# Four taps of the 31-tap convolution in each TensorE product instead of two, the taps divided anew over the engines, and the kernel's opening reordered

## The reference

```python
def pool_mixer(h, w, b, scale):               # windows 2, 4, 8, 16: running mean minus the value itself
    csum = jnp.cumsum(hf, axis=1)
    ...
        mean = (c - lo) / count[None, :, None]
        outs.append(mean - hf[..., sl])
    p = jnp.stack(outs, axis=2).astype(h.dtype)
    y = jnp.einsum('bsgc,gcd->bsgd', p, w) + b
    return y.reshape(B, S, D) * scale

def conformer_conv(x, w_in, b_in, conv_w, conv_b, ln_g, ln_b, w_out, b_out):
    a, g = jnp.split(x @ w_in + b_in, 2, axis=-1)
    h = a * jax.nn.sigmoid(g)
    h = lax.conv_general_dilated(             # depthwise, 31 taps, causal, 1024 channels
        h, conv_w[:, None, :].astype(h.dtype), window_strides=(1,),
        padding=[(CONV_KERNEL - 1, 0)],
        dimension_numbers=("NWC", "WIO", "NWC"),
        feature_group_count=D_MODEL) + conv_b
    h = jax.nn.silu(layer_norm(h, ln_g, ln_b))
    return h @ w_out + b_out
```

## Time and profile before

| | |
|---|---|
| median of 3 runs | 1448.52 us |
| profiled execution | 1448.29 us |
| its span (first to last instruction) | 1446.5 us |
| TensorE busy / VectorE / ScalarE / GpSimd | 1437.2 / 921.2 / 637.3 / 204.8 us |
| convolution stage, 929.4 to 1040 us: busy of the same four | 109.79 / 106.03 / 99.21 / 96.55 us of 110.6 |
| its DMA share (mean busy share of 16 engines) | 0.71 |

### The profile page before, as it was taken

How to read it: one execution, slowest core, us unless ns; L and a number is a source line. 1 busy time by engine, 2 the same in 40 slices (tenths; PEclk the granted TensorE clock), 3 DMA queues, 4 the chain that set the end, 5 groups by cost and what they waited for, 6 DMA issues and landing times.

```text
span 1446.5 us, 19954 instructions
## 1 busy us (share of the span) xinstructions
PE 1437.2 (99%) x6828; PEld 1172.1 (81%) x6828; DVE 921.2 (64%) x1339; ACT 637.3 (44%) x994; POOL 204.8 (14%) x162
## 2 busy tenths in 40 slices
PE   9999999999999999999999999999999999999999
PEld 8788888888887898888888888766588888888887
DVE  7877773573645667777754755899988653544532
ACT  7444442342546675444422434798754321222210
POOL 4000000000302232000000003599511000000000
PEclk9999999999999999999999999999999999999999
DMA  5223223222322112232232232387613332222321
GB/s 191 88 99 104 87 102 116 73 102 91 121 90 71 30 60 81 96 108 94 91 125 75 88 108 81 101 186 179 161 45 102 116 101 89 100 102 88 102 94 51
DMA packets 44413, 144.34 MB, mean 100 GB/s; under 512 B 5184, under 2 KB 6208, under 8 KB 44352
## 3 DMA queue, kind: packets, MB, share of 16 engines
q1 hardware_dynamic: 41200, 133.79, 28.0%
q0 software_dynamic: 2016, 7.34, 2.8%
q10 hardware_dynamic: 1136, 2.42, 0.4%
HBM read 137.19 MB, written 2.10 MB: 96 GB/s over the span
## 4 chain that ended last, share of the span: by engine, by line
PE 94%; DVE 2%; ACT 1%; DMA 1%; issue 1%; POOL 1%; SPq 0%; ACTq 0%; DVEq 0%; POOLq 0%
PE bank L594 29%; PE bank L595 29%; PE bank L596 29%; PE bank L867 2%; PE bank L742 1%; PE bank L770 1%; PE bank L755 1%; DVE bank L1689 1%; PE bank L877 0%; DMA cst<-cst_in 0%; DMA shifted<-hc 0%; PE bank L922 0%; PE bank L923 0%; PE bank L635 0%; PE bank L926 0%
## 5 line engine op out<-in xcount | busy, mean ns | idle before, releaser
L594 PE MATMUL bank<-xh,whi 128*128 128x512 f32 x1184 | 464.9, 393 | 0.8 <-DVE wlo L1340 0.6
L596 PE MATMUL bank<-xh,wlo 128*128 128x512 f32 x1184 | 460.9, 389 | 0.0
L595 PE MATMUL bank<-xl,whi 128*128 128x512 f32 x1184 | 460.8, 389 | 0.0
L945 ACT ACTIVATE whi<-raw 128x1024 fp32r<-128x1024 f32 x244 | 255.8, 1050 | 238.7 <-PE bank L596 236.0
L1340 DVE TENSOR_TENSOR wlo<-raw,whi 128x1024 fp32r<-128x1024 f32 x230 | 288.0, 1252 | 43.8 <-ACT whi L945 35.9
L594 PEld LDWEIGHTS bank<-xh,whi 128*128 128x128 f32 x1184 | 222.2, 188 | 55.4 <-issue 7.1
L595 PEld LDWEIGHTS bank<-xl,whi 128*128 128x128 f32 x1184 | 222.3, 188 | 46.6 <-issue 1.2
L596 PEld LDWEIGHTS bank<-xh,wlo 128*128 128x128 f32 x1184 | 222.3, 188 | 46.4
L594 PE MATMUL bank<-ahi,whi 128*128 128x512 f32 x608 | 236.5, 389 | 0.0
L595 PE MATMUL bank<-alo,whi 128*128 128x512 f32 x608 | 236.5, 389 | 0.0
L596 PE MATMUL bank<-ahi,wlo 128*128 128x512 f32 x608 | 236.5, 389 | 0.0
(11 more groups left out here) (191 smaller groups left out, 1344.6 us busy)
## 6 DMA issues: line engine op xcount, KB each, us to landing
raw<-w_ffn_up SPq DMA_DIRECT2D x88, 512.0 KB, 3.3
raw<-w_ffn_down SPq DMA_DIRECT2D x32, 512.0 KB, 3.2
raw<-w_mlp_up SPq DMA_DIRECT2D x32, 512.0 KB, 3.2
raw<-w_mlp_down SPq DMA_DIRECT2D x32, 512.0 KB, 3.2
raw<-w_ain SPq DMA_DIRECT2D x16, 512.0 KB, 3.4
raw<-w_ffn_down SPq DMA_DIRECT2D x16, 384.0 KB, 3.0
raw<-w_qkv SPq DMA_DIRECT2D x12, 512.0 KB, 3.2
wlo<-w_ain POOLq DMA_DIRECT2D x10, 512.0 KB, 7.3
```

The source lines that it names most:

```text
L594: nc.tensor.matmul(out_, hi, mh, start=first, stop=False)
L595: nc.tensor.matmul(out_, hi, ml, start=False, stop=False)
L596: return nc.tensor.matmul(out_, lo, mh, start=False, stop=last)
L945: nc.scalar.activation(whi[:, s, 0:tiles * P], raw[:, s, 0:tiles * P], ACT.Copy)\
```

## The change

1. **TensorE's products** hold four taps: 32 channels, four times on the partitions, each copy one token later. A round is four matmuls of 32 output columns, for four taps of 128 channels. Taps on TensorE go from 68 to 92 and rounds from 34 to 23 (4, 3, 3, 2, 3, 3, 7, 9 become 2, 2, 2, 2, 2, 3, 5, 5).
2. **The shifted copies** of a chunk are still four DMAs, one per group of 32 channels; each reads its 32 rows four times, overlapping, and writes all 128 partitions: 512 runs of some 2 KB instead of 256.
3. **The diagonals** are made by VectorE, one instruction per chunk, from a table `pair_w4` that 16 DMAs of short runs (17 numbers, 68 bytes) write before the attention; before, ScalarE did it in 68 instructions.
4. **The taps** elsewhere: own 56 to 51, late 52 to 42, GpSimd's 72 to 63. The last `gated` stands behind all taps of its round and `collect(5)`. Places of the adding DMAs move.
5. **`statistics`** is four matmuls of 32 columns over half the tokens each, instead of two of 64 over all.
6. **The opening**: no products with zeros, the window matrices made on GpSimd without the constants' DMA, the residual's bias on GpSimd, two loads moved from ScalarE's queue to SP's, `weigh_pooled` on VectorE no longer waiting for ScalarE's half, 8 instead of 10 warm-up products, two splits moved.

```diff
-PE_TAPS = (8, 6, 6, 4, 6, 6, 14, 18)
-SHIFTS = 2
-GROUP = P // SHIFTS
+PE_TAPS = (8, 8, 8, 8, 8, 12, 20, 20)
+SHIFTS = (4,) * C
+GROUP = tuple(P // s for s in SHIFTS)
+ROUNDS = tuple(n // s for n, s in zip(PE_TAPS, SHIFTS))
...
-DIAGS = 3
-POOL_TAPS = (11, 10, 9, 9, 9, 9, 8, 7)
-LATE_TAPS = (0, 6, 8, 11, 11, 12, 4, 0)
-LATE_START = (2, 2, 2, 0, 0, 0, 0, 4)
+DIAGS = 2
+POOL_TAPS = (10, 9, 9, 8, 8, 8, 7, 4)
+LATE_TAPS = (2, 4, 6, 9, 12, 9, 0, 0)
+LATE_START = (2, 2, 2, 0, 0, 0, 0, 0)
...
-LOW_AT = {... 17: (7, 3), 18: (7, 6), 19: (7, 6)}
+LOW_AT = {... 17: (6, 5), 18: (7, 1), 19: (7, 3)}
...
-WARM = 10
+WARM = 8
@@ load_pairs
+                    for s in range(shifts):
+                        for g in range(shifts):
+                            src = vec_in[g * group:(g + 1) * group, w:w + C * TAPS].rearrange("p (c k) -> p c k", c=C)
+                            sp.dma_start(pair_w[shifts][s:P:shifts, g], src[:, lo:hi, s:s + n]).then_inc(pairs_loaded, 16)
@@ shift_hc
-                for g in range(SHIFTS):
-                    for s in range(SHIFTS):
-                        sp.dma_start(shifted[s * GROUP:(s + 1) * GROUP, c % 2, g, 0:n],
-                                     hc[g * GROUP:(g + 1) * GROUP, c % HC, s:s + n]).then_inc(hc_shifted[c % 2], 16)
+                for g in range(SHIFTS[c]):
+                    window = hc[g * group:(g + 1) * group, c % HC, 0:n]
+                    taps = bass.AP(window.tensor, window.offset, [window.ap[0], (1, SHIFTS[c]), (1, n)])
+                    sp.dma_start(shifted[:, c % 2, g, 0:n], taps).then_inc(hc_shifted[c % 2], 16)
@@ SP's loads of the opening
+                    sp.dma_start(res[:, 6:8, :], xT[:, 6:8, :]).then_inc(x_in[3], 16)
+                    sp.dma_start(vec[:, head:], vec_in[:, head:]).then_inc(vec_loaded, 16)
@@ GpSimd
+            for c in range(C):
+                pool.wait_ge(chain_done, 2 * (c // 2) + 2)
+                nc.gpsimd.tensor_scalar(res[:, c, :], res[:, c, :], col(pbs, c), None, ALU.add).then_inc(res_biased, 1)
@@ window_mean
-                nc.tensor.matmul(bank[BAND_BANKS[c]][:], zero[:, 0:P], zero[:], start=True, stop=False)
...
-                                          start=False, stop=(b == NBLK - 1))
+                                          start=(b == 0), stop=(b == NBLK - 1), skip_group_check=True)
@@ convolve
+                for q in range(ROUNDS[c]):
+                    for g in range(SHIFTS[c]):
+                        rows, at = slice(g * group, (g + 1) * group), SHIFTS[c] * q
+                        mm = nc.tensor.matmul(bank[6 + b][rows, :], dg[:, c % DIAGS, q, rows],
+                                              shifted[:, b, g, at:at + T],
+                                              start=(q == 0), stop=(q == ROUNDS[c] - 1))
@@ statistics
+                for j, x in enumerate((hv[:, c, :], sq[:, c % 2, :])):
+                    for h in range(2):
+                        rows, at = slice((2 * j + h) * QUADRANT, (2 * j + h + 1) * QUADRANT), slice(h * T // 2, (h + 1) * T // 2)
+                        mm = nc.tensor.matmul(norm[0][rows, at], ones[:, 0:QUADRANT], x[:, at],
+                                              start=(c == 0), stop=(c == C - 1))
@@ VectorE, once per chunk behind gated(c)
+                V.tensor_tensor(dg[:, c % DIAGS, 0:rounds].rearrange("p q (g n) -> p q g n", g=shifts),
+                                pair_id[shifts][:].rearrange("p (q g n) -> p q g n", q=1, g=1).broadcast_to(shape),
+                                w.rearrange("p g (q n) -> p q g n", n=1).broadcast_to(shape), ALU.mult)\
+                    .then_inc(diag_ready, 1)
...
-                    if n == gated_at and c == C - 2:
-                        gated(C - 1)
...
+                if c == C - 2:
+                    gated(C - 1)
```

More of the change, by code:

```diff
@@ L188, in build @@
             wg = sb("wg", [P, 4, 2, 2 * P], F32, own)
-            near = sb("near", [P, 5, PAD + P + PAD], F32, own)
+            near = sb("near", [P, 5, P + PAD], F32, own)
             mix = sb("mix", [P, 2, 4, P + PAD], F32, own)
             mixed = sb("mixed", [P, NBLK, 4, P + PAD], F32, own)
-            zero = sb("zero", [P, T], F32R, own)
             pick = sb("pick", [P, NBLK, NBLK], F32, own)
@@ L997, in step @@
                             k = 2 * b + j
-                            split_hi(p.unit, i, k + AHEAD)
-                            if first and isinstance(i, int) and i == 0 and k == 0:
+                            opening = first and isinstance(i, int) and i == 0
+                            if not (opening and k == 1):
+                                split_hi(p.unit, i, k + AHEAD)
+                            if opening and k == 0:
                                 root(first)
+                                split_hi(p.unit, i, 1 + AHEAD)
                             par = VEC["glu"] + ((layer * FF_PAIRS + q0) * 2 + k) * 4 + 16 * i
@@ L1218, in _ @@
             p = ph["ain"]
-            def diagonals(c, part=0, parts=1):
-                if c >= DIAGS and part == 0:
-                    act.wait_ge(conv_done, c - DIAGS + 1)
-                if c == 0:
-                    act.wait_ge(pairs_loaded, 16 * SHIFTS * (SHIFTS + 1))
-                pairs = PE_TAPS[c] // SHIFTS
-                for q in range(part * pairs // parts, (part + 1) * pairs // parts):
-                    e = c * TAPS + SHIFTS * q
-                    for g in range(SHIFTS):
-                        last = nc.scalar.activation(dg[:, c % DIAGS, q, g, :], pair_id[:], ACT.Copy,
-                                                    scale=pair_w[:, g, e:e + 1])
-                if part == parts - 1:
-                    last.then_inc(diag_ready, 1)
             def products(c, ks):
@@ L1400, in step @@
                         par = VEC["glu"] + ((layer * FF_PAIRS + q0) * 2 + 2 * b) * 4 + 16 * i
+                        opening = first and isinstance(i, int) and i == 0 and b == 0
                         split_lo(p.unit, i, 2 * b + AHEAD)
-                        if first and isinstance(i, int) and i == 0 and b == 0:
+                        if opening:
                             invert(first, rinv_count)
@@ L1414, in step @@
                                                        op0=ALU.mult, op1=ALU.add).then_inc(done, 1)
[L1415 removed]
+                        if not opening:
+                            split_lo(p.unit, i, 2 * b + 1 + AHEAD)
                         dve.wait_ge(gate_ready, pair + 1)
@@ L1531, in add_pooled @@
                                        op0=ALU.mult, op1=ALU.add).then_inc(pooled, 1)
-            for g in range(4):
-                weigh_pooled(g)
+            weigh_pooled(0)
+            window_weights()
+            weigh_pooled(1)
+            first_window_weights()
+            weigh_pooled(2)
+            weigh_pooled(3)
             evict_pooled(0)
@@ L1543, in _ @@
             V.tensor_tensor(square_of(4), square_of(4), square_of(0), ALU.add).then_inc(all_summed, 1)
-            window_weights()
-            split_lo(0, 0, 4)
+            for m in range(C):
+                for half in range(2):
+                    h = C * (m // REP) + REP * half + m % REP
+                    made = V.memset(qs[HD * half:HD * (half + 1), m:m + 1], HD ** -0.5 / SLOPE[h])
+            made.then_inc(q_scales, 1)
             dve.wait_ge(rms_ready, 1)
@@ L1756, in _ @@
                 gate_at = next((n for n in range(rounds) if issued[n] >= GATE_AT), rounds - 1)
-                gated_at = next((n for n in range(rounds) if issued[n] >= LAST_GATED), rounds - 1)
                 for n in range(rounds):
```

180 lines of the change are left out of this document (82 added, 98 removed).

## The result

The changed kernel takes 1457.61 us (median of 4 runs, 1454.63 to 1459.89) beside 1448.53 us for the kernel before: a ratio of 1.0057, with a 95% interval of 1.0044 to 1.0070. It is slower by 6 to 10 us, where 1440.9 was forecast. The profiled run is its fastest, 1454.63 us with a span of 1452.6, so the trace explains 6.1 us more of span than before; the rest of the median's distance lies in how the other runs vary.

What follows compares the result with a forecast made beforehand. TensorE was busy 1437.2 of 1446.5 us, but the convolution stage's end hung on VectorE, four DMAs, `convolve(7)` and the last statistics. 1448.5 - 3.8 (stage) - 3.8 (opening) = 1440.9; range 1436.0 to 1446.5, the forecast's own 1437.5 to 1443.5.

Steps and rivals of the forecast that it cites:

- The bound of before: End of the convolution stage: the path is VectorE, four DMAs, `convolve(7)`, the last statistics.
- A round at 0.85 us: TensorE's convolution: four column groups run at once, so 23 rounds cost 19.6 us, 9.4 less than the old 34.
- VectorE up to `gated(7)`: Convolution stage: taps -5.5, `collect(5)` +1.4, diagonals +5.1, waits for TensorE -1.3; sum -0.3 us.
- The copies of chunk 7: Ahead of `convolve(7)`: twice the bytes in twice the runs, +2.2 us, landing at 1031.6; bounds +0 and +5.
- The last product: `convolve(7)` on TensorE: 5 rounds instead of 9, 4.5 us instead of 7.90, ending at 1036.1.
- Behind it: After `convolve(7)`: only addition 0.69, square 0.63 and statistics 0.5 follow, where 3.8 us stood; layer norm at 1038.1.
- The opening: Kernel start: earlier loads, no products with zeros and fewer waits, -4.4 us at best; -3.8 after 0.6 for the clock.
- The warm-up: Opening: a gap of over 1 us before L683 could lower TensorE's clock; 2.2 us lost at worst, 0.6 taken.
- The tables: Before the attention: 17 issues, 10.4 us, delay a qkv load to about 377.5, needed at 383.13; price 0, bound +3.
- The second one: Convolution stage: DMA engines become the bound, `shifted` waits at `convolve(1)` to `(6)` over 4 us; 1444.7, up to 1448; chance 0.23.
- The first rival: TensorE's whole gain comes through, 16.8 us, with no idle time ahead of `convolve(7)`: 1431.9; chance 0.10.
- the third: Convolution on TensorE: four groups of 32 columns don't run at once, 1.70 us a round, 1454.9; chance 0.06.

Runs made afterwards that it cites:

- half_runs: The whole change with each run of a shifted copy cut to some 1 KB, second half of tokens left out, for timing only: 1445.93 us, ratio 0.9973.
- loads_wait: low_late, with SP issuing the three 512 KB weight loads only after the copies of chunk 7 have landed: 1452.70 us, ratio 1.0026.
- low_late: The whole change with the adding DMAs of blocks 17 to 19 moved behind the third sum of chunk 7: 1453.79 us, ratio 1.0025.
- last_four: Kernel before with the change's opening and statistics, four taps for chunk 7 only, adding DMAs 17 to 19 late, overlapping copies: 1447.15 us, ratio 0.9979.
- split_queue: last_four with two of the four copies of chunk 7 issued by ScalarE's queue instead of SP's: 1445.94 us, ratio 0.9977.
- last_four_warm: last_four with 12 matmuls of ones (some 2.8 us) on TensorE ahead of `convolve(7)`: 1445.43 us, ratio 0.9971.

## Why the prediction was wrong, step by step

**The bound of before** was read rightly at the end (VectorE, four copies, `convolve(7)`), but the transfers were taken as a latency on that path and not as a resource that was nearly used up.

**A round at 0.85 us**: right. The passes of the two long products at the high clock differ by (5.36 - 4.50) / 8 = 0.107 us, 0.86 us for eight. Four groups of 32 columns run at once; the Trainium skill's 2.38x ("TensorE: Matmul & The Clock Gate", "Part 3: Packing small matmuls"), by which it would have been 1.07, doesn't fit this trace. Statistics are 0.54 us a chunk in the middle of the stage (970.66 to the next product at 971.20), where about 0.5 was taken.

**VectorE up to `gated(7)`, -0.3 forecast, +2.6 measured.** The diagonals were right: seven instructions took 0.42, 0.43, 1.05, 0.42, 0.59, 1.01 and 0.82 us, 4.7 in sum, where 5.1 was taken. The error is the last term, "-1.3 us of waits for TensorE that go". They grew from 1.3 to 3.5 us, since TensorE waited 2.25 and 4.45 us for the copies of chunks 0 and 1. With half the bytes they were zero and the step took 95.4 us, 0.2 more than before (half_runs): near the forecast's sum, once the copies don't hold TensorE.

**The copies of chunk 7 are the step that failed.** It priced doubled bytes as +2.2 us, "bounds +0 and +5"; measured, from output to product, +7.4. The working took 34.9% of 6.4 us as the copies' cost, read where they were alone on the engines, and added as much. What else would be on the engines it put at nothing in the sum. The runs show from output to product:

| what runs beside the copies of chunk 7 | us | run |
|---|---|---|
| old bytes, nothing | 4.75 | before |
| half of the new bytes, adding DMAs and loads | 5.25 | half_runs |
| twice the bytes, next to nothing | 7.6 | loads_wait |
| twice the bytes, three loads | 8.5, 8.0 | low_late, last_four |
| twice the bytes, loads and adding DMAs | 12.1 (to 12.9 in three more traces) | whole change |

Twice the bytes alone are +2.9 (+2.2 forecast), the company beside small copies is +0.5, and both together are +7.4. So the bytes were priced nearly well, and the cost that was missing, some 4 us, arises where the larger copies and the other transfers meet: most of it (3.6, low_late) goes with the adding DMAs, the loads' part is 0.9 or less. That is why either cure works, half the bytes (half_runs) or no adding DMAs beside them (low_late). The issues are a part of the 2.9: two queues instead of one gave 1.2 us in last_four's form. The diff of `LOW_AT` showed that the adding DMAs of blocks 17 to 19 had moved forward, 18 and 19 ahead of the last sums of chunk 7; a collision with them stood in the bounds and belonged in the sum.

**The last product**, -3.4 forecast, -0.7 measured: its 40 passes took 7.23 us and not 4.5. The missing 2.7 us are the clock, 0.50 after 9.3 us of idle time. The prediction weighed the clock in the opening, where it was idle for a moment, and left it out where it forecast 3 to 6 us of idle time itself. **Behind it** -1.9 was forecast and -1.5 measured.

**The opening**, -3.8 forecast, about -2 measured. The first product starts at 5.57, even earlier than forecast, but all 64 passes of L700 end at the time of before:

```profile
5.57 7.53 PE L700 MATMUL bank<-wg,res 128*128 128x256 f32 x32 [0.46 <-DMA res<-xT]
13.76 3.69 PE L700 MATMUL bank<-wg,res 128*128 128x256 f32 x16 [0.66 <-DVE zT L1483]
...
18.36 3.70 PE L700 MATMUL bank<-wg,res 128*128 128x256 f32 x16
21.89 7.47 PE L725 MATMUL bank<-mixed,zT 128*128 128x129 f32 x64
```

In the earlier trace rows the product behind these 64 passes starts at 21.94, here at 21.89, so the start that is 1.5 us earlier is given back. A wait of 0.66 us for `zT` is a part of it, and the first 32 passes took 7.53 us, where 32 at 0.22 are 7.0. The inputs are still arriving (the DMA share is 0.80 in the first 20 us, 0.79 before); that they set this pace is likely and not shown. The products with zeros gave 2.0 us of the 2.4. The warm-up needed no price: 7.53 us for 32 passes is 0.235 each, near those 0.22 of the high clock. The bias on GpSimd took 15.0 us where I had 8 x 1.3, and started at 13.7 instead of 9, since it stands behind all of ScalarE's squares, which end at 13.5.

**The tables**: no wait appeared before the attention, price 0 was right, 68-byte runs and all.

**The rivals.** The second one came true in kind: a DMA share of 0.89 (0.90 was worked out) and waits for copies at chunks 0, 1 and 4, 5.2 us of them at `convolve(1)` and `(4)`, where over 4 was its sign. It was capped at 1448, because it let the lost time eat the stage's gain and no more. Nothing limits it there: a wait in the last product is paid in full, plus the clock. The first rival fell with the wait of 9.35 us, the third with a round of 0.86 us. (The first one's time has a slip: 1448.5 - 16.8 is 1431.7 and not 1431.9.) The chance of 0.23 and the 0.06 on "slower" were both too small for a trace that showed a share of 0.71 to which a quarter was to be added.

**Left open:** why the whole change varies by 5 us between runs while the kernel before varied by 1 beside it; and how much of the middle waits (7.4 us) comes from the larger copies and how much from adding DMAs beside them. No run moved the adding DMAs of chunks 0 to 5. Open too are what the new statistics and the new form of the copies give by themselves, which by last_four's trace may be 2.5 us.

## What to carry to other kernels

When an edit buys engine time with bytes, price the bytes at the share that the DMA engines have in that stage, and look in the order for every transfer that lands beside the one on the path: here 0.71 plus a quarter turned -3.8 into +7.8 us. Price a transfer together with what runs beside it: here bytes alone cost 2.9 us, company alone 0.5 and both 7.4. When a variant of several parts wins, look in the trace where: the version with four taps in one chunk gained 2.5 of its 3.3 us in chunks that have two. A forecast of idle time on TensorE is a forecast of a lower clock for what comes behind it, and a few useless products in that gap are worth trying; here they kept the clock up in two traces, but no gain in the median was shown.

## What the runs showed of the hardware

- Four column groups of 32 ran at once (the change, last_four): 0.107 us a pass for 128x512 f32, as for two groups 0.2125.
- The clock after idle time on TensorE, in the convolution stage: after 9.3 us (the change) and 5.4 us (half_runs) the product began at 0.50. After 1.9 us (split_queue) and 4.7 us (loads_wait) it was still 1.00 in the gap and low when the product had begun (0.50 and 0.52). After 3.15 us in last_four's profiled run it stayed at 1.00. The length of the gap alone did not decide it.
- The granted clock reads 1.00 in the first 5.57 us of the change's trace, though the opening's warm-up passes of 128 columns took 3.79 us for 16, 0.237 each, and the same passes in last_four_warm 2.95 us for 24, 0.123 each. At the start the time of a pass says more than that row.
- Four DMAs in a row on SP's queue, each reading 32 rows four times and writing 128 partitions (264 KB), took 4.21 us to issue, four plain ones of 64 partitions (132 KB) 2.39. It isn't the form: in last_four the first two took 0.60 each and the next two 1.33 and 1.80, and with two on each of two queues (split_queue) SP's two took 1.25 together.
- A VectorE product of two broadcast SBUF operands took 0.42 to 1.05 us for 256 elements and 0.82 for 640.
- GpSimd's addition of a column to 128x512 took 1.88 us on average in the opening, and its three additions of two tiles there 1.27 each.
